# Weight sums for a seven-product up projection: made ahead in DRAM instead of on VectorE, with other banks, buffers and chain slots

## The chip, the cores and the metric

One core of a Trainium2 chip runs the whole program. The metric is the device time of one execution in microseconds (us). TensorE (PE), VectorE (DVE), ScalarE (ACT), GpSimd (POOL) and SyncE (SP) each work through an instruction list of their own, in order, and wait on semaphores; SP and POOL here only issue DMAs.

## The reference

Two transformer blocks are applied to 1024 tokens of width 1024, all in float32. Block one mixes tokens by an RWKV scan and differential attention, block two by a Fourier mix and a gated convolution. The change is in what follows in both of them, and this part reads, in the reference's names:

```
x = x + gt1 * rmsnorm(y, g_post_mix)            # y = mixer output @ w_out
h = modulate(rmsnorm(x, g_pre_ffn), sh2, sc2)   # second block: rmsnorm only
u = dwconv(h @ w_up, ffn_conv) + ffn_conv_b     # w_up is 1024 x 5632, 3 taps over the tokens
val, gate = split(u, 2)                         # second block: gate first, gelu
x = x + gt2 * rmsnorm((val * silu(gate)) @ w_down, g_post_ffn)
```

The first block also needs `silu(c) @ w_mod`, whose later part is summed on DVE while the RWKV scan runs.

## The kernel before, in words

The program is a row of stages: first block's input and projection, the RWKV scan (`rwkv`), attention, and then one long stage with four parts: first mixer (`mixer_out_to_ffn`, "mix1"), its down projection followed by the second block's input jobs and Fourier mix (`DownToMerge`), second mixer ("mix2", the same function), and the last down projection.

Every float32 matmul is done as three: an operand is split into a rounded high part (ACT, `weight_high`, L3402) and the remainder (DVE, `weight_low`, L3407), and high x high, low x high and high x low are added up in PSUM (L3586 to L3588).

A mixer has 186 steps on PE, each with one weight piece of 512 columns (four 128x128 blocks) and 12 matmuls of 512 tokens (24 of 258 in mix2). `plan_steps` writes them down in order:

- Steps 0 to 31, kind "O": 16 output tiles of `w_out`, first token half and then second. For each half a chain of norm work (`chain(a, e)` on PE, ACT and DVE, with e the step counted from the half's start) runs beside the 16 steps that follow: sums of squares, `means`, `spreads`, eight `residual` rows, squares again, `means`, `scale_rows`, and on ACT `shift_rows` (first block only). The chain of half 1 runs beside steps 32 to 47.
- Steps 32 to 47, "early": products P1 and P2 for the eight tiles in `EARLY` = 3, 5, 7, 9, 0, 1, 11, 13. These need only half 0 of h.
- The rest, "late": 22 tiles of h @ w_up, each a value and a gate tile of 128 columns. A tile is computed as a 2x2 block product (tokens and depth each halved) with seven products in place of eight: P1, P6, P7, P5, P2, P4, P3. The early tiles have five left. So there are 8 tiles of five steps and 14 of seven: tiles 0 and 1 have five, tiles 2 to 13 alternate between seven and five, and tiles 14 to 21 have seven.

The seven products want sums and differences of the operands. On the token side they are the "turns" t1 to t4 (`add_turns`, then rounded by `round_turns` on ACT and `low_turns` on DVE), made once before the late steps. On the weight side they are made for every tile on DVE: `add_weights` (L3423, L3425, L3426) and one more sum in `weight_low` (L3415). ACT's `weight_high` of a summed piece waits for the sum.

What a product leaves in PSUM is taken by DVE (`take`, L3856 to L3864, one for each of P6, P7, P5, P4, P3). ACT then scales the centre tap (`centre_gate` after P4's take, `centre_val` after P3's), DVE adds the outer taps (`tap`, L3870), ACT applies the activation, and DVE multiplies (L3888). The result goes to DRAM and is read back for the down projection.

The order of the work is written by hand. At step s, ACT first splits the weights of step s + 3, then does that step's own work; DVE does taps or product, the low split of step s + 3, taps, and last `take(s)`, which waits for PE to end step s. Four ring buffers hold the split weights. Raw weights come in four buffers of 512 KB (8 depth blocks, so a pair of pieces each), loaded by SP and freed after the last use. PSUM banks of the late steps are fixed by kind (`late_bank`): P7 and P4 of a tile share a bank, so P4 waits until DVE has taken P7 (`took`), and PE cannot start P4 until then. PE waits for `w_low` before every step.

## Time and profile before

| | us |
|---|---|
| median of 3 runs | 3728.32 (3721.13 to 3732.64) |
| the profiled execution | 3724.28 |
| its span in the trace | 3722.4 |

| engine | busy us | share of span | instructions |
|---|---|---|---|
| PE | 3406.6 | 92% | 30711 |
| DVE | 2404.7 | 65% | 3809 |
| ACT | 1582.8 | 43% | 2735 |
| POOL | 182.5 | 5% | 335 |

The median of the runs is the time to be compared; the profiled execution, 4.04 us below it, is where all durations below come from. Its span leaves out 1.88 us around it. The page gives busy time by engine, the span in 40 slices with the granted clock of TensorE, the chain of work that ended last, and the costliest groups of instructions with the idle time before them and what ended it. A matmul's listed duration overlaps the next one's, so the pace of PE is read from start to start, and its idle time from the bracket ahead of a matmul.

In time the parts lie about so: RWKV scan 490 to 1010, attention to 1300, mix1 1300 to 1980, down projection to 2250, second block's input and Fourier mix to 2770, mix2 to 3440, last down projection to the end. In the RWKV stage's window the DMA engines are busy for a share of 0.32; the busiest of the page's 40 slices moved 262 GB/s.

### The profile page before, as it was taken

What the parts mean: (1) busy time and instruction counts of PE and PEld (TensorE: products, weight loads), DVE (VectorE), ACT (ScalarE), POOL (GpSimd) and SP (SyncE); (2) the same over time, 40 slices, a digit from 0 to 9 for tenths busy, and PEclk for the clock granted to TensorE, in tenths of its full rate; (3) what the DMA queues carried; (4) which work ended last, traced back from release to release, by engine and by line L of the source; (5) the groups of instructions that cost most, each with busy time, mean ns of one, the idle gap of its engine ahead of it and who ended that gap; (6) DMA issues with size and microseconds to landing.
All of it is one profiled execution on the core that took longest, in us unless ns stands there. A gap on an engine that the chain in (4) does not pass through costs nothing.

```text
span 3722.4 us, 73022 instructions
## 1 busy us (share of the span) xinstructions
PE 3406.6 (92%) x30711; PEld 3081.6 (83%) x30711; DVE 2404.7 (65%) x3809; ACT 1582.8 (43%) x2735; POOL 182.5 (5%) x335
## 2 busy tenths in 40 slices
PE   7999999999989897788898999999999788898999
PEld 4787789888877775666668999899999788898999
DVE  5477778878757746777776884322235777777565
ACT  4556644444347634333334553111134333334454
POOL 2000000000000010000000111000000000000110
PEclk9999999999889999899999999999999899999999
DMA  6234442323233052222325763111123222232774
GB/s 241 71 128 139 140 163 97 112 92 96 55 74 87 1 162 87 63 68 79 95 69 192 262 216 122 29 35 46 49 85 117 80 70 84 69 91 84 261 239 159
DMA packets 328479, 410.36 MB, mean 110 GB/s; under 512 B 15795, under 2 KB 255894, under 8 KB 328152
## 3 DMA queue, kind: packets, MB, share of 16 engines
q1 hardware_dynamic: 298184, 306.49, 26.9%
q0 software_dynamic: 29968, 99.19, 8.2%
q8 instruction: 244, 4.00, 0.5%
q14 instruction: 83, 0.68, 0.1%
HBM read 322.68 MB, written 82.94 MB: 109 GB/s over the span
## 4 chain that ended last, share of the span: by engine, by line
PE 38%; DVE 14%; issue 4%; DVEq 3%; ACT 3%; DMA 2%; ACTq 0%; POOL 0%
PE psum L3586 5%; PE psum L3588 4%; PE psum L3587 4%; PE psum L2846 4%; PE psum L2847 4%; PE psum L2848 4%; PE psum L2369 3%; PE psum L2371 3%; PE psum L2370 3%; DVE mix_u_val L3870 3%; DVE mix_u_gate L3870 2%; DMA down_w_raw<-in_w_down 2%; DVE mix_w_split L3407 2%; ACT mix_w_split L3402 2%; PE psum L2705 1%
## 5 line engine op out<-in xcount | busy, mean ns | idle before, releaser
L2235 DVE TENSOR_TENSOR down_w_lo<-down_w_raw,down_w_hi 128x1024 fp32r<-128x1024 f32 x228 | 270.5, 1186 | 442.2 <-ACT down_w_hi L2209 440.1
L3586 PE MATMUL psum<-mix_t_hi,mix_w_split 128*128 128x258 f32 (+1 forms) x1056 | 358.2, 339 | 145.6 <-DVE mix_x_gate L3858 86.2
L2209 ACT ACTIVATE down_w_hi<-down_w_raw 128x1024 fp32r<-128x1024 f32 x228 | 234.6, 1029 | 572.0 <-PE psum L2848 328.4
L2369 PE MATMUL psum<-down_ghi,down_w_hi 128*128 128x256 f32 x1408 | 404.5, 287 | 12.4 <-DVE down_glo L2240 12.2
L2371 PE MATMUL psum<-down_glo,down_w_hi 128*128 128x256 f32 x1408 | 399.7, 284 | 0.0
L2370 PE MATMUL psum<-down_ghi,down_w_lo 128*128 128x256 f32 x1408 | 399.5, 284 | 0.0
L3586 PEld LDWEIGHTS psum<-mix_t_hi,mix_w_split 128*128 128x128 f32 x1056 | 211.0, 200 | 180.7 <-DVE mix_w_split L3407 106.1
L3587 PE MATMUL psum<-mix_t_hi,mix_w_split 128*128 128x258 f32 (+1 forms) x1056 | 351.2, 333 | 0.0
L3588 PE MATMUL psum<-mix_t_lo,mix_w_split 128*128 128x258 f32 (+1 forms) x1056 | 350.8, 332 | 0.0
L3407 DVE TENSOR_TENSOR mix_w_split<-mix_w_raw,mix_w_split 128x512 fp32r<-128x512 f32 x240 | 165.1, 689 | 212.2 <-ACT mix_w_split L3402 211.9
L2369 PEld LDWEIGHTS psum<-down_ghi,down_w_hi 128*128 128x128 f32 x1408 | 271.6, 193 | 14.5 <-DVE down_glo L2240 14.1
L2370 PEld LDWEIGHTS psum<-down_ghi,down_w_lo 128*128 128x128 f32 x1408 | 271.8, 193 | 0.3
L2371 PEld LDWEIGHTS psum<-down_glo,down_w_hi 128*128 128x128 f32 x1408 | 271.5, 193 | 0.0
L2846 PE MATMUL psum<-h_hi,down_w_hi 128*128 128x348 f32 (+2 forms) x768 | 249.1, 324 | 0.6 <-DVE h_lo L2533 0.6
L2847 PE MATMUL psum<-h_hi,down_w_lo 128*128 128x348 f32 (+2 forms) x768 | 247.1, 322 | 0.0
L2848 PE MATMUL psum<-h_lo,down_w_hi 128*128 128x348 f32 (+2 forms) x768 | 246.9, 321 | 0.0
L3588 PEld LDWEIGHTS psum<-mix_t_lo,mix_w_split 128*128 128x128 f32 x1056 | 210.4, 199 | 17.5
L3587 PEld LDWEIGHTS psum<-mix_t_hi,mix_w_split 128*128 128x128 f32 x1056 | 211.3, 200 | 15.9
L3402 ACT ACTIVATE mix_w_split<-mix_w_sum 128x512 fp32r<-128x512 f32 x132 | 82.4, 624 | 315.4 <-DVE mix_w_sum L3426 242.2
L757 PE MATMUL psum<-h_hi,w_hi 128*128 128x512 f32 (+1 forms) x536 | 209.3, 390 | 0.7 <-DVE w_lo L923 0.7
L758 PE MATMUL psum<-h_hi,w_lo 128*128 128x512 f32 (+1 forms) x536 | 199.4, 372 | 0.0
L759 PE MATMUL psum<-h_lo,w_hi 128*128 128x512 f32 (+1 forms) x536 | 199.3, 372 | 0.0
(501 smaller groups left out, 8676.5 us busy)
## 6 DMA issues: line engine op xcount, KB each, us to landing
down_w_raw<-in_w_down SPq DMA_DIRECT2D x176, 512.0 KB, 4.3
mix_w_raw<-in_w_up SPq DMA_DIRECT2D x104, 512.0 KB, 5.3
g_scratch<-mix_u_val POOLq DMA_DIRECT2D x44, 512.0 KB, 4.0
down_w_raw<-in_w_in SPq DMA_DIRECT2D x36, 512.0 KB, 4.0
down_g_part<-g_scratch POOLq DMA_DIRECT2D x6, 2816.0 KB, 17.2
rw_operands<-step_set SPq DMA_DIRECT2D x16, 1024.0 KB, 6.4
mod_w<-in_w_mod POOLq DMA_DIRECT2D x32, 512.0 KB, 5.6
mix_w_raw<-in_w_out SPq DMA_DIRECT2D x32, 512.0 KB, 4.0
```

Source lines behind the costliest of these rows:

```text
L2209: self.nc.scalar.activation(self.hi[s][:, 0:w], self.raw[s][:, 0:w], ACT.Copy).then_inc(self.w_high, 1)
L2235: last = self.nc.vector.tensor_tensor(self.lo[s][:, 0:w], self.raw[s][:, 0:w], self.hi[s][:, 0:w].bitcast(F32), ALU.subtract)
L2369: nc.tensor.matmul(out, w_hi[:, w], g_hi[:, :], start=(n == 0 and c % 2 == 0), stop=False, skip_group_check=True)
L2370: nc.tensor.matmul(out, w_lo[:, w], g_hi[:, :], start=False, stop=False, skip_group_check=True)
L2371: last = nc.tensor.matmul(out, w_hi[:, w], g_lo[:, :], start=False, stop=(n == KF - 1), skip_group_check=True)
L2846: nc.tensor.matmul(out, w_hi[:, w], x_hi[:, xk, x], start=(kk == 0), stop=False)
L2847: nc.tensor.matmul(out, w_lo[:, w], x_hi[:, xk, x], start=False, stop=False)
L2848: last = nc.tensor.matmul(out, w_hi[:, w], x_lo[:, xk, x], start=False, stop=end)
L3407: nc.vector.tensor_tensor(ring[s % 4][:, 1, :], src, ring[s % 4][:, 0, :].bitcast(F32), ALU.subtract).then_inc(w_low.sem, 1)
L3586: nc.tensor.matmul(out, w[:, 0, c], xh[:, x], start=(first and kk == 0), stop=False, skip_group_check=True)
L3587: nc.tensor.matmul(out, w[:, 1, c], xh[:, x], start=False, stop=False, skip_group_check=True)
L3588: last = nc.tensor.matmul(out, w[:, 0, c], xl[:, x], start=False, stop=(kk == 3), skip_group_check=True)
```

## The change

Five things are changed, all for both mixers.

1. Four sums of `w_up` (1024 x 2816 each in use: 512 rows) are made by DMA in DRAM, in tensors `up_sums`. `sum_weights` issues them on POOL: 16 copies of 1408 KB, then 16 transfers of 1408 KB that add to what they write (`accum_op=ALU.add`), with waits on semaphores between dependent ones. Mixer 0's 32 transfers stand one behind each of the 32 loads of `w_mod` in the RWKV stage; mixer 1's stand behind the tables of the Fourier mix, ahead of POOL's last wait before mix2. DVE's four weight sums per tile are gone. SP waits for all sums of its mixer before the first late load.
2. Raw weights come one piece per step (256 KB) in ten buffers, instead of two pieces in four: 186 loads per mixer instead of 68.
3. The late steps' PSUM banks are handed out by longest unused (`slot_of`, `freed_by`) among all eight (four pairs in mix2).
4. The final rows of half 0 are written where t1 and t4 will be made (`final`) and stay there whole, so that `add_turns` has four additions for each kk instead of six.
5. The chain of half 1 has two residual rows per step (e = 3 to 6) and its own slots: second `means` at e = 8 (before 11), `scale_rows` at e = 10 and 11 (before 13 and 14), `add_turns` spread over e = 11 to 14 (before all of it at 14 and 15), and `low_turns` one kind per step from e = 15 on (before three kinds at e = 15).

The semaphores of the down projection's first rows are also cut from five to three.

```diff
@@ rwkv, gpsimd
                 pool.dma_start(k.mod_w[i % 3][:, :], w_mod[:, kk, c:c + MOD_COLS]).then_inc(mod_landed[i % 3], 16)
+                sum_weights(pool, k, 0, i)
@@ DownToMerge.gpsimd
+        for i in range(32):
+            sum_weights(pool, self.k, 1, i)
         pool.wait_ge(self.used, self.total)
@@
+def sum_weights(pool, k, mixer, at):
+    j, c = divmod(at, 4)
...
+    if j < 4:
+        src = (w[low, gate], w[low, val], w[low, val], w[high, val])[j]
+        pool.dma_start(sums[j, low, :], src).then_inc(done, 16)
+    elif j < 6:
+        src = (w[high, gate], w[low, gate])[j - 4]
+        pool.wait_ge(done, base + 64)
+        pool.dma_start(sums[(0, 2)[j - 4], low, :], src, accum_op=ALU.add, max_dma_last_dim=5632).then_inc(done, 16)
+    else:
+        pool.wait_ge(done, base + 16 * j)
+        pool.dma_start(sums[(1, 3)[j - 6], low, :], sums[(0, 1)[j - 6], low, :],
+                       accum_op=ALU.add, max_dma_last_dim=5632).then_inc(done, 16)
@@ mixer_out_to_ffn
+    for s in range(first_late, STEPS):
+        kind, i = steps[s]
+        if kind in ("P2", "P3"):
+            slot = slot_of["P1" if kind == "P2" else "P5", i]
+        else:
+            slot = min(range(SLOTS), key=lambda j: last_use[j])
+            freed_by[kind, i] = user.get(slot)
...
     def weight_high(act, s):
-        kind, i = steps[s][0:2]
-        src, r = source(s)
-        if kind in SUM and not early(s):
-            act.wait_ge(*w_added.at(4 * i + SUM[kind]))
-        else:
-            act.wait_ge(*w_landed[r % 4].at(landed_at(r)))
+        act.wait_ge(*w_landed[s % RAWS].at(landed_at(s)))
...
     def weight_low(dve, s):
-        if s + 1 < STEPS and s + 1 >= first_late:
-            kind, i = steps[s + 1]
-            if kind == "P6":
-                add_weights(dve, i)
-            elif kind == "P4":
...
     def sync(sp):
-        for r in range(TILES):
-            if r >= 4:
-                sp.wait_ge(*w_low.at(released[r - 4]))
+        for s in range(STEPS):
+            if s >= RAWS:
+                sp.wait_ge(*w_low.at(s - RAWS + 1))
...
+            if s == first_late:
+                for done in k.sums_done:
+                    sp.wait_ge(done, 128 + 128 * spec["mixer"])
@@ tensor, bank_free
-            elif kind == "P4":
-                pe.wait_ge(*took.at(5 * i + 2))
...
+            elif not early(s) and kind != "P2" and freed_by[kind, i]:
@@ vector, chain of half 1
+            elif a == 1:
+                if 3 <= e <= 6:
+                    residual(a, 2 * e - 6, 2 * e - 5)
+                elif e == 8:
+                    means(a, 1)
+                elif e in (10, 11):
+                    scale_rows(a, 4 * e - 40)
+                    if e == 11:
+                        add_turns(0)
+                elif 12 <= e <= 14:
+                    add_turns(e - 11)
+                elif e == 15:
+                    low_turns("t2")
@@ vector, add_turns
-            tt(f["t1"], h0[0][kk][:, :].bitcast(F32), b12, ALU.subtract)
+            tt(f["t1"], f["t1"], b12, ALU.subtract)
             tt(f["t3"], b12, b22_row, ALU.subtract)
-            dve.drain()
-            tt(f["t1"], f["t1"], h0[1][kk][:, :].bitcast(F32), ALU.add)
```

On DVE, in a late tile of seven steps, from one pair of value taps to the gate taps (mix_w_split is the split weights' ring, mix_w_sum the weight sums, mix_u and mix_x_* what is taken from PSUM). Before:

```order
L3870 SCALAR_TENSOR_TENSOR mix_u_val<-mix_x_val_18160,prm,mix_u_val 128x1024 x2
L3407 TENSOR_TENSOR mix_w_split_18167<-mix_w_raw_18164,mix_w_split_18167 128x512
L3415 TENSOR_TENSOR mix_w_sum_18171<-mix_w_raw_18164,mix_w_sum_18171 128x512
L3856 TENSOR_TENSOR mix_u_18151<-psum,mix_x_val_18161 128x512
L3888 TENSOR_TENSOR mix_u_val<-mix_u_val,mix_u_gate 128x1024
L3407 TENSOR_TENSOR mix_w_split_18168<-mix_w_raw_18165,mix_w_split_18168 128x512
L3858 TENSOR_TENSOR mix_x_gate<-mix_u_18151,psum 128x512
L3407 TENSOR_TENSOR mix_w_split_18169<-mix_w_sum_18171,mix_w_split_18169 128x512
L3860 TENSOR_TENSOR mix_x_gate<-mix_x_gate,psum 128x512
L3407 TENSOR_TENSOR mix_w_split_18166<-mix_w_raw_18162,mix_w_split_18166 128x512
L3423 TENSOR_TENSOR mix_w_sum_18170<-mix_w_raw_18163 128x512
L3425 TENSOR_TENSOR mix_w_raw_18163<-mix_w_raw_18163,mix_w_raw_18162 128x512
```

And in the changed kernel:

```order
L3877 SCALAR_TENSOR_TENSOR mix_u_val<-mix_x_val_18211,prm,mix_u_val 128x1024 x2
L3434 TENSOR_TENSOR mix_w_split_18224<-mix_w_raw_18214,mix_w_split_18224 128x512
L3863 TENSOR_TENSOR mix_u_18202<-psum,mix_x_val_18212 128x512
L3895 TENSOR_TENSOR mix_u_val<-mix_u_val,mix_u_gate 128x1024
L3434 TENSOR_TENSOR mix_w_split_18225<-mix_w_raw_18215,mix_w_split_18225 128x512
L3865 TENSOR_TENSOR mix_x_gate<-mix_u_18202,psum 128x512
L3434 TENSOR_TENSOR mix_w_split_18226<-mix_w_raw_18216,mix_w_split_18226 128x512
L3867 TENSOR_TENSOR mix_x_gate<-mix_x_gate,psum 128x512
L3434 TENSOR_TENSOR mix_w_split_18223<-mix_w_raw_18217,mix_w_split_18223 128x512
L3434 TENSOR_TENSOR mix_w_split_18224<-mix_w_raw_18218,mix_w_split_18224 128x512
```

The order of splits, takes and taps is the same; the weight sums (L3415, L3423, L3425, and L3426 just behind) are no longer between them.

On DVE at the end of mix1's early steps, from the first four scaled rows (L3776, now L3783) on; mix_t_sum and mix_t_lo are the turns and their low parts. Before, after all four kk:

```order
L3799 TENSOR_TENSOR mix_t_sum<-mix_y_18148,mix_t_sum 128x512
L3801 TENSOR_TENSOR mix_t_sum<-mix_h_18116,mix_t_sum 128x512
L3803 TENSOR_TENSOR mix_t_sum<-mix_t_sum,mix_h_18116 128x512
L3812 TENSOR_TENSOR mix_t_lo<-mix_t_sum,mix_t_hi 128x512 x4
L3812 TENSOR_TENSOR mix_t_lo<-mix_t_sum,mix_t_hi_18123 128x512
L3812 TENSOR_TENSOR mix_t_lo<-mix_t_sum,mix_t_hi_18124 128x512
L3812 TENSOR_TENSOR mix_t_lo<-mix_t_sum,mix_t_hi_18125 128x512
L3812 TENSOR_TENSOR mix_t_lo<-mix_t_sum,mix_t_hi_18126 128x512
L3812 TENSOR_TENSOR mix_t_lo<-mix_t_sum,mix_t_hi 128x512 x4
L3407 TENSOR_TENSOR mix_w_split_18169<-mix_w_raw_18163,mix_w_split_18169 128x512
```

In the changed kernel:

```order
L3801 TENSOR_TENSOR mix_t_sum<-mix_t_sum,mix_y_18199 128x512
L3802 TENSOR_TENSOR mix_t_sum<-mix_y_18199 128x512
L3804 TENSOR_TENSOR mix_t_sum<-mix_y_18199,mix_t_sum 128x512
L3806 TENSOR_TENSOR mix_t_sum_18176<-mix_t_sum_18176,mix_t_sum 128x512
L3434 TENSOR_TENSOR mix_w_split_18225<-mix_w_raw_18213,mix_w_split_18225 128x512
L3815 TENSOR_TENSOR mix_t_lo<-mix_t_sum,mix_t_hi 128x512 x4
L3434 TENSOR_TENSOR mix_w_split_18226<-mix_w_raw_18214,mix_w_split_18226 128x512
L3815 TENSOR_TENSOR mix_t_lo<-mix_t_sum,mix_t_hi 128x512 x4
```

The low parts of one kind of turn now stand between two weight splits, where before twelve stood in a row ahead of one.

On POOL in the RWKV stage (mod_w are the three buffers of `w_mod` pieces), the start of the changed kernel's list; before, only the L1289 rows stand there:

```order
L1289 DMA mod_w_4212<-in_w_mod 128x1024
L3265 DMA up_sums<-in_w_up 128x2816
L1289 DMA mod_w_4213<-in_w_mod 128x1024
L3265 DMA up_sums<-in_w_up 128x2816
L1289 DMA mod_w_4214<-in_w_mod 128x1024
L3265 DMA up_sums<-in_w_up 128x2816
```

Each load of `w_mod` now has a transfer of 1408 KB ahead of it in POOL's queue.

## Rows read from the trace of the kernel before

**Rows 1.** What PE waited for, 1300:2000, then 2760:3450: us in total, times, longest
```profile
PE psum L3586 <- DVE mix_x_gate L3858: 47.4, 19, 5.7
PE psum L3586 <- ACT mix_x_val L3680: 23.8, 1, 23.8
...
PE psum L3586 <- ACT mix_x_val L3680: 22.6, 1, 22.6
```
**Rows 2.** Timeline of PE in mix1: start, us, engine, line, operands, count, [idle before]
```profile
1656.39 0.77 PE L3586 MATMUL psum<-mix_t_hi,mix_w_split 128*128 128x512 f32 x1 [5.28 <-DVE mix_x_gate L3858]
...
1661.65 0.63 PE L3586 MATMUL psum<-mix_b_hi,mix_w_split 128*128 128x512 f32 x1
...
1855.10 0.40 PE L3586 MATMUL psum<-mix_b_hi,mix_w_split 128*128 128x512 f32 x1
...
1863.50 0.40 PE L3586 MATMUL psum<-mix_t_hi,mix_w_split 128*128 128x512 f32 x1
```
**Rows 3.** Timeline of DVE, one late tile of seven steps in mix1
```profile
1844.56 2.64 DVE L3870 SCALAR_TENSOR_TENSOR mix_u_val<-mix_x_val,prm,mix_u_val 128x1024 f32<-128x1024 f32 x2
...
1847.90 0.69 DVE L3415 TENSOR_TENSOR mix_w_sum<-mix_w_raw,mix_w_sum 128x512 f32<-128x512 f32 x1
...
1854.15 0.69 DVE L3423 TENSOR_TENSOR mix_w_sum<-mix_w_raw 128x512 f32<-128x512 f32 x1
...
1856.93 0.69 DVE L3407 TENSOR_TENSOR mix_w_split<-mix_w_sum,mix_w_split 128x512 fp32r<-128x512 f32 x1 [0.70 <-ACT mix_w_split L3402]
...
1860.24 0.69 DVE L3407 TENSOR_TENSOR mix_w_split<-mix_w_raw,mix_w_split 128x512 fp32r<-128x512 f32 x1 [1.83 <-ACT mix_w_split L3402]
...
1867.07 2.64 DVE L3870 SCALAR_TENSOR_TENSOR mix_u_val<-mix_x_val,prm,mix_u_val 128x1024 f32<-128x1024 f32 x2
```
**Rows 4.** The chain that ended last: first gate tap of tiles 1, 13, 21; mix2's 1, 21
```profile
1536.53 1.28 DVE mix_u_gate L3870
...
1793.52 1.28 DVE mix_u_gate L3870
...
1971.07 1.28 DVE mix_u_gate L3870
...
2997.19 1.28 DVE mix_u_gate L3870
...
3432.19 1.28 DVE mix_u_gate L3870
```
**Rows 5.** Timelines of PE, then DVE, where mix1's late steps begin
```profile
1495.80 0.77 PE L3586 MATMUL psum<-mix_t_hi,mix_w_split 128*128 128x512 f32 x1 [23.76 <-ACT mix_x_val L3680]
...
1463.94 0.69 DVE L3407 TENSOR_TENSOR mix_w_split<-mix_w_sum,mix_w_split 128x512 fp32r<-128x512 f32 x1 [0.79 <-ACT mix_w_split L3402]
...
1469.42 0.69 DVE L3407 TENSOR_TENSOR mix_w_split<-mix_w_raw,mix_w_split 128x512 fp32r<-128x512 f32 x1 [2.21 <-ACT mix_w_split L3402]
...
1483.10 0.69 DVE L3794 TENSOR_TENSOR mix_t_sum<-mix_h,mix_y 128x512 f32<-128x512 f32 x1
...
1487.57 0.69 DVE L3794 TENSOR_TENSOR mix_t_sum<-mix_h,mix_y 128x512 f32<-128x512 f32 x1
...
1516.73 2.65 DVE L3870 SCALAR_TENSOR_TENSOR mix_u_gate<-mix_x_gate,prm,mix_u_gate 128x1024 f32<-128x1024 f32 x2
```
**Rows 6.** Timeline of POOL in the RWKV stage: loads 15 and 31 of 0 to 31
```profile
710.58 0.53 POOL L1289 DMA_DIRECT2D mod_w<-in_w_mod  x1 [25.26 <-DVE mod_sum L1575]
...
919.33 0.53 POOL L1289 DMA_DIRECT2D mod_w<-in_w_mod  x1 [21.19 <-DVE mod_sum L1575]
```
**Rows 7.** Timeline of POOL, the end of the Fourier tables and mix2's first loads
```profile
2764.11 2.15 POOL L3451 DMA_DIRECT2D mix_temp<-x_scratch  x4 [480.23 <-PE psum L2848]
```
**Rows 8.** DMA issues of the page: count, KB each, median us from issue to landing
```profile
mix_w_raw<-in_w_up SPq DMA_DIRECT2D x104, 512.0 KB, 5.3
...
mod_w<-in_w_mod POOLq DMA_DIRECT2D x32, 512.0 KB, 5.6
...
dft_cos<-in_dft_cos_k POOLq DMA_DIRECT2D x1, 1042.0 KB, 6.7
```

More of the change, by code:

```diff
@@ L2138, in __init__ @@
         self.part_rows = [k.at(f"{name}_part_rows{s}", [20, PART], (86528, 43136)[s]) for s in range(2)]
-        self.first_landed = [sem(f"{name}_first_rows_landed{j}") for j in range(5)]
+        self.first_landed = [sem(f"{name}_first_rows_landed{j}") for j in range(3)]
         self.part_landed = [None] + [sem(f"{name}_part_landed{p}") for p in range(1, SEQ // PART)]
@@ L3250 @@
     pass
+def sum_weights(pool, k, mixer, at):
+    j, c = divmod(at, 4)
+    w, active_first = ((k.ins["w_up"][0], False), (k.ins["w_up_2"][0], True))[mixer]
+    val, gate = (slice(FF, 2 * FF), slice(0, FF)) if active_first else (slice(0, FF), slice(FF, 2 * FF))
+    sums, done, base = k.up_sums[mixer], k.sums_done[c], 128 * mixer
+    low, high = slice(P * c, P * c + P), slice(512 + P * c, 512 + P * c + P)
+    if j < 4:
[9 more added lines that the diff above has]
+                       accum_op=ALU.add, max_dma_last_dim=5632).then_inc(done, 16)
 class Counted:
@@ L3320, in mixer_out_to_ffn @@
     xv = lambda i: stash[X_BUFFER[i]]
-    fresh = [i for i in range(KF) if i not in EARLY]
-    kept_before = lambda i: max([QUEUE] + [KEPT[j] + 1 for j in fresh if j <= i - SETS])
     low_cols, high_cols = slice(dst, dst + n), slice(dst + n, dst + 2 * n)
@@ L3428, in sync @@
-    def sync(sp):
-        for r in range(TILES):
-            if r >= 4:
-                sp.wait_ge(*w_low.at(released[r - 4]))
-            elif before and r < 2:
-                sp.wait_ge(before.low, before.total - 1 + r)
+        nc.vector.tensor_tensor(ring[s % 4][:, 1, :], raw[s % RAWS][:, :], ring[s % 4][:, 0, :].bitcast(F32),
+                                ALU.subtract).then_inc(w_low.sem, 1)
+    def sync(sp):
+        for s in range(STEPS):
+            if s >= RAWS:
+                sp.wait_ge(*w_low.at(s - RAWS + 1))
+            elif before and s < 4:
+                sp.wait_ge(before.low, before.total - 1 + s // 2)
@@ L3569, in tensor @@
             a, e = chain_of(s)
-            first = kind in ("P1", "P6", "P7", "P5") or (kind == "O" and steps[s][2] == 0)
+            first = kind not in ("P2", "P3") and (kind != "O" or steps[s][2] == 0)
             for j in range(nb):
@@ L3574, in tensor @@
                 else:
-                    out = k.psum[:, late_bank(i, BANK[kind], j), 0:pw]
+                    out = k.psum[:, late_bank(i, kind, j), 0:pw]
                 if kind == "P2":
@@ L3777, in scale_rows @@
                 else:
-                    nc.vector.scalar_tensor_tensor(out=row, in0=row, scalar=gain_pre(order[a][j]), in1=spread_out[:, 0:n],
+                    nc.vector.scalar_tensor_tensor(out=final(a, order[a][j]), in0=row, scalar=gain_pre(order[a][j]), in1=spread_out[:, 0:n],
                                                    op0=ALU.mult, op1=ALU.mult).then_inc(scaled.sem, 1)
@@ L3951, in four_tiles, with mixer_memory @@
     return [k.at(f"{name}{j}", [n], places[j], dt)[:, :] for j in range(4)]
-def mixer_memory(k, name, n, first, ring_at, spots):
+def mixer_memory(k, name, n, first, ring_at, first_spots, later_spots):
     at = k.at
@@ L3959, in mixer_memory @@
     h0 = [[first_rows[:, kk // 4, q, kk % 4, :] for kk in range(KD)] for q in range(2)]
-    spots = iter(spots)
+    first_spots, later_spots = iter(first_spots), iter(later_spots)
     turn, turn_f32 = {}, {}
-    for which in ("t1", "t2", "t3", "t4", "b22"):
-        places = [[next(spots) for _ in range(4)] for _ in range(2)]
+    for which in ("t1", "t4", "t2", "t3", "b22"):
+        lasting = which in ("t1", "t4")
+        places = [[next(first_spots if lasting and q else later_spots) for _ in range(4)] for q in range(2)]
         turn[which] = [four_tiles(k, f"{name}_{which}_{p}", n, places[q], F32R) for q, p in enumerate(("hi", "lo"))]
@@ L4089, in program @@
         k.x_dram = nc.dram_tensor("x_scratch", [KD, P, SEQ], F32, kind="Internal").ap()
+        k.up_sums = [nc.dram_tensor(f"up_sums{m}", [4, 512, FF], F32, kind="Internal").ap() for m in range(2)]
+        k.sums_done = [k.lasting(f"up_sums_done{c}") for c in range(4)]
         k.g_dram = nc.dram_tensor("g_scratch", [KF, P, SEQ], F32, kind="Internal").ap()
```

213 lines of the change are left out of this document (95 added, 118 removed).

## The prediction

> **What bounds the kernel now.** I read the busy shares first: PE is at 92%, so the gain can only lie in its gaps. The windows by part show where they are: the late steps of both mixers and the passage into them. PE's waits name the cause [rows 1]: in mix1 47.4 us for L3858, DVE's take of P7, and one wait of 23.8 us as the late steps begin; in mix2 the latter is 22.6. P4 uses P7's bank and stands behind that take, and the take stands behind taps and splits in DVE's list, so the question is who sets the pace, the bank or DVE.
>
> PE's own pace: 36 matmuls (three steps) lie between the last two rows of [rows 2], 8.40 us, 0.233 each (the 2.4 GHz level), so a step is 2.80 us, a tile of seven 19.6, a tile of five 14.0. The chain that ended last shows the real pace [rows 4]: tiles 1 to 13, six pairs of a seven and a five, take 257.0 us, 42.8 a pair where PE needs 33.6; tiles 13 to 21 take 177.55 us, 22.2 each where PE needs 19.6. Tiles 1 to 21 take 434.5 us in mix1 and 435.0 in mix2.
>
> DVE's timeline of a seven-step tile [rows 3] has a period of 22.51 us, and DVE waits in it only for ACT: 0.70 us once and 1.83 us twice. The 1.83 is a loop: take, ACT's centre tap, ACT's high split, DVE's low split, and nothing in DVE's list lies between. DVE is the bound, and the waits of [rows 1] are how PE learns of it.
>
> **The late steps.** Removed on DVE per tile: L3415, 0.78 us to the next start, and from 1854.15 to the split at 1856.93, 2.78 us of three sums and the 0.70 wait for the last [rows 3]. Together 3.56.
> - Seven steps: 22.51 - 3.56 = 18.95 us of DVE, under PE's 19.6. PE becomes the bound. DVE may fall some 6 us behind inside a tile (gate taps and both loops come at its end), but splits are made three steps = 8.4 us ahead, so this is just covered. I take 19.65 a tile: tiles 13 to 21 take 157.2 us, 20.3 less.
> - A pair: 42.8 less twice 2.95 us of sums (2.17 for the three, 0.78) and about 0.5 of waits for them leaves 36.4, over PE's 33.6. DVE stays the bound, since both loops stay in the five-step tile, and PE idles some 2.8 us a pair. Six pairs: 218.4 us, 38.6 less.
> - Tile 0 to 1: 19.8 us ([rows 4, 5]) becomes about 17.5, 2.3 less.
> That is 61 in mix1. Mix2's matmuls are 516 columns a step against 512, so PE's part is 1% longer and I take 59.
>
> The new banks remove the wait by name, not the bound: a bank is reused four steps or more later in mix2, nine or more in mix1 after tile 1, and a split that PE needs for step s is in DVE's list behind the take of step s - 4. So the bank wait costs nothing, and gives nothing beyond the DVE time counted.
>
> **The passage into the late steps.** Before, PE ended its early steps and idled 23.76 us, to 1495.80 [rows 5]. DVE's chain slot with the first scaled rows begins at 1463.94 and lasts 5.48 us to 1469.42 (shift on ACT, then its split); it leads to PE's start 31.9 us later. Six additions of a kk took 4.47 us (1483.10 to 1487.57); four take about 3.1. In the changed list, from the same slot on: 5.5, then 6.4 (four rows, additions of one kk, split), three times 3.85, and 1.4 for a split and the first low part of t2: 24.8 us. But the slot now comes at e = 10, with six steps of PE's left, 17.0 us with a spread, where it came with three. It can begin 1.0 us after that step. So PE idles 25.8 - 17.0 = 8.8 us. What PE did for sums in steps 10 and on moves ahead, so the slot starts 1.8 us later against the old place than the steps alone say: P6 starts at about 1479.9, 15.9 us earlier. Tile 0 then has one kind of low turns per step and is paced by DVE at about 4 us a step, as long as before to its gate taps. In mix2, which has no shift on ACT, the idle of 22.6 becomes about 8, and tile 0 gets some 3 shorter: 17. Two residual rows per step cost nothing themselves (3.5 us of DVE in a step of PE's of 2.8 us and two sums); what they bring is the earlier slot.
>
> **Loads.** Seven loads of 256 KB per tile replace two of 512 KB. A 512 KB load takes 5.3 us to land [rows 8]; ten buffers let a load start some six steps, 16 us, before ACT wants it. Nothing on the path. At 2.65 us each one after the other, seven would take 18.6 of 19.6 us, so only if nothing overlapped would this be near. By the Trainium skill ("DMA: Bandwidth & Descriptors", Anatomy of one DMA) a DMA costs about 2.0 us fixed plus bytes at 436 GB/s: an estimate by it is 2.6 us for 256 KB, the same answer. No run here shows 256 KB of `w_up` alone.
>
> **The sums by DMA.** No row shows an accumulating or a DRAM to DRAM transfer. For 1408 KB, bounds by the nearest rows: 1042 KB landed in 6.7 us, 512 KB in 5.6 [rows 8], so 9.1 to 15.4 for a move of that size with its latency, and up to twice the lower, 18.1, if an addition reads a second stream at that pace. Below, latency is paid once in a full queue: 1408 KB at the 262 GB/s of the profile's busiest slice is 5.5. I take 9 for an addition, nearest to the 1042 KB row, and 6 for a copy.
>
> Mixer 0: the 16 additions go with loads 16 to 31 of `w_mod`, from 710.58 to 919.33 [rows 6], 208.7 us, beside 16 loads of some 2.5 us of queue time. No delay up to (208.7 - 40) / 16 = 10.5 us an addition, about 11.8 with the loads' lead of one pair (some 20 us). With 9 the cost is nothing; the DMA engines are busy for only 32% of that window. I put 3 us on contention with the scan's loads. Could it gain? No, nothing is taken out there.
>
> Mixer 1: POOL was idle for 480.23 us before its loads of x at 2764.11 [rows 7]. 16 copies of 6 and 16 additions of 9 are 240 us. Hidden up to about (480 - 96) / 16 = 24 us an addition. The weight loads beside them, one of at most 512 KB per job of some 11 us, are issued two jobs ahead, so even twice their time to land is covered.
>
> **Sum.** 3724.28 - (15.9 + 61) - (17 + 59) + 3 = 3574. The median of the runs lies 4 above the profiled execution, so 3578, 4.0% less than 3728.
>
> **Rivals.**
> 1. PE gains only half of it. Late tiles of seven steps have 0.65 us of slack against DVE; if their stalls do not vanish, and PE falls to half clock after each stall of a pair, the gain melts. Behind a stall of 5.28 us 12 matmuls took 5.26 us, 0.44 each (the 1.2 GHz level), against 0.233 [rows 2]: 2.4 us more, and for each of 12 pairs 29 us. With 0.7 us more in each of 28 seven-step tiles, 20 us, this gives about 3578 + 49 = 3627. For it: that stall comes in a pair of tiles, and pairs keep a stall. Against it: by the sum it is 2.8 us and not 5.28, and DVE sets the pair's length, so a slower PE is partly hidden.
> 2. The additions are slow and hold up the scan: slower than before. POOL's queue is first in, first out, so a load of `w_mod` stands behind an addition; DVE's mod sums wait for it, and with them in DVE's list the scan. Each us over 11.8 costs 16. At 18.1 us (the bound above) it is 100 us, 3678; from 21.2 us on the change loses, and at 24, 195 us, the time is 3773. For it: twice the reading and an addition in the DMA engine, with no row that says otherwise. Against it: bytes alone give 9. The Trainium skill ("DMA: Bandwidth & Descriptors", Queues, rings and completion order) has descriptors of one ring consumed in order, which is the rule this rests on; that no later load overtakes is not shown in this trace.
> 3. The seven-product steps are held by the weights from DRAM: SP's wait for `sums_done` before the first late load. In mix2, at more than 24 us an addition, both x and late weights come late. It joins rival 2.
>
> **Chances.** Forecast 0.66, rival 1 0.21, rival 2 (with 3) 0.13, of which 0.08 is slower than before and 0.05 lies between. 3578 is the forecast's; its own range is 3555 to 3605. The range for 8 in 10 goes to rival 1: 3548 to 3642. Runs of this kernel tell 0.3% (11 us) from no change: faster 0.90, same 0.02, slower 0.08.
>
> **What would show it.** Right: gate taps 19.6 to 19.8 us apart in tiles 14 to 21 and 36 to 37 a pair; no wait for a take, but waits for the low split (now L3434), in five-step tiles; one wait of 7 to 10 us where P6 begins; the scan's stage still 520 us long; POOL past its additions before 2764. Wrong: DVE waiting for `mod_w` or DMA issues on POOL stretched after 710 (rival 2); PE stalls over 3 us with matmuls 0.43 us apart in each pair (rival 1); tiles of seven above 20.3.

## The result, and the profile after

| | us |
|---|---|
| changed kernel, median of 4 runs | 3829.07 (3825.76 to 3833.37) |
| kernel before, beside them, median of 4 runs | 3730.48 |
| ratio | 1.0268, 95% interval 1.0245 to 1.0291 |
| span of the profiled execution | 3827.1 (before 3722.4) |

The change makes the kernel 2.7% slower; 4.0% faster was forecast. The span cut at five instructions that all kernels here have shows where it went. The marks are DVE's first product of the attention stage, ACT's first weight split of mix1, PE's first transposition of the meta rows (some 10 us behind mix1's last gate row), ACT's first split of mix2, and SP's last store. In brackets stands the time between the stores of gate rows 0 and 21, the late steps.

| kernel | to the attention | attention | mix1 (late) | down, second input | mix2 (late), last down |
|---|---|---|---|---|---|
| before | 1056.8 | 249.3 | 685.2 (450.6) | 766.9 | 959.3 (451.1) |
| after | 1179.7 | 248.0 | 623.3 (406.9) | 876.8 | 894.9 (405.0) |
| difference | +122.9 | -1.3 | -61.9 | +109.9 | -64.4 |

So the mixers gained 126 us of the 153 forecast, and the two places where the sum transfers run, costed at 3 us together, lost 233. The windows by part show the same (us, busy time of each engine with its instructions, granted clock, DMA share, GB/s), of the kernel before:
```profile
485.00:1010.00 525.00, 488.02 (x11926) 460.75 (x11925) 407.67 (x905) 216.84 (x576) 16.93 (x32) 0.95 0.32 103
...
2250.00:2500.00 250.00, 250.00 (x1495) 233.39 (x1496) 82.50 (x127) 52.45 (x78) 9.57 (x17) 1.00 0.17 52
```
and of the changed one:
```profile
485.00:1134.00 649.00, 518.80 (x11962) 488.99 (x11962) 405.63 (x901) 213.62 (x578) 43.30 (x64) 0.87 0.53 153
...
2311.00:2600.00 289.00, 192.59 (x1050) 174.71 (x1049) 60.39 (x108) 39.72 (x66) 34.13 (x49) 0.82 0.75 195
2600.00:2940.00 340.00, 339.87 (x2148) 339.66 (x2147) 87.69 (x87) 61.44 (x71) 2.20 (x4) 1.00 0.17 48
```
In the scan the instructions are nearly the same and the stage is 124 us longer, at a DMA share of 0.53 where it was 0.32. In the second block's input part PE, busy all the time before, idles 96 of 289 us, while the 32 transfers of mixer 1 run; once they are through, it is at 100% again.

**What waits there.** First the waits of the scan window, then those of the input part (us in total, times, longest):
```profile
POOL mod_w L1289 <- DVE mod_sum L1576: 353.6, 25, 35.6
...
ACT kb L1728 <- DMA unit<-rw_values: 135.8, 12, 16.5
ACT kb L1728 <- DMA unit_first<-rw_values: 51.3, 6, 15.7
```
```profile
DVE down_w_lo L2236 <- ACT down_w_hi L2210: 191.3, 10, 40.5
ACT down_w_hi L2210 <- DMA down_w_raw<-in_w_in: 109.8, 4, 38.8
...
PE psum L2849 <- DVE down_w_lo L2236: 35.8, 1, 35.8
```
POOL waits for DVE, as before [rows 6]; DVE never waits for `mod_w`. The scan waits for its own operands, which SP loads: 18 waits, 187 us, where the kernel before had 5 and 5.6 us. These loads have a short lead (the time from issue to need), as one of them shows: SP's issue, then ACT's first use, before:
```profile
606.91 0.62 SPq L1254 DMA_DIRECT2D unit_first<-rw_values  x1
...
612.41 0.63 ACT L1727 ACTIVATE kb<-unit_first 128x512 f32<-128x512 f32 x1 [0.44 <-DMA unit_first<-rw_values]
```
after:
```profile
626.67 1.08 SPq L1254 DMA_DIRECT2D unit_first<-rw_values  x1
...
640.88 0.63 ACT L1728 ACTIVATE kb<-unit_first 128x512 f32<-128x512 f32 x1 [9.15 <-DMA unit_first<-rw_values]
```
In both, ACT is ready for the load some 5 us after its issue (5.5 - 0.44 and 14.2 - 9.15), so whatever it takes beyond that is waited for. The DMA issues of the scan window (count, KB each, median us to landing), before (`mod_w` is in [rows 8]):
```profile
unit<-rw_operands SPq DMA_DIRECT2D x22, 512.0 KB, 5.0
...
unit<-rw_values SPq DMA_DIRECT2D x26, 128.0 KB, 5.9
```
after:
```profile
up_sums<-in_w_up POOLq DMA_DIRECT2D x24, 1408.0 KB, 12.4
mod_w<-in_w_mod POOLq DMA_DIRECT2D x32, 512.0 KB, 7.3
unit<-rw_operands SPq DMA_DIRECT2D x22, 512.0 KB, 16.4
up_sums<-up_sums POOLq DMA_DIRECT2D x8, 1408.0 KB, 16.9
...
unit<-rw_values SPq DMA_DIRECT2D x26, 128.0 KB, 15.7
```
and in the input part after, 2311 to 2600:
```profile
up_sums<-in_w_up POOLq DMA_DIRECT2D x24, 1408.0 KB, 41.0
up_sums<-up_sums POOLq DMA_DIRECT2D x8, 1408.0 KB, 29.1
down_w_raw<-in_w_in SPq DMA_DIRECT2D x12, 512.0 KB, 37.9
```
of which the kernel before, 2285 to 2760, had:
```profile
down_w_raw<-in_w_in SPq DMA_DIRECT2D x28, 512.0 KB, 4.0
```
What is on POOL's own queue suffers little (5.6 to 7.3 us). What SP issues beside it does: a unit's 512 KB take 16.4 us instead of 5.0, its 128 KB 15.7 instead of 5.9, and a block of `w_in` 37.9 instead of 4.0.

**The late steps.** Two timelines of one pair in mix1 (start, us, engine, line, operands, idle before), PE, then DVE:
```profile
1709.44 0.39 PE L3589 MATMUL psum<-mix_t_lo,mix_w_split 128*128 128x512 f32 x1
1713.38 0.77 PE L3587 MATMUL psum<-mix_b_hi,mix_w_split 128*128 128x512 f32 x1 [3.54 <-DVE mix_x_gate L3867]
...
1718.62 0.39 PE L3587 MATMUL psum<-mix_h,mix_w_split 128*128 128x512 f32 x1
```
```profile
1709.84 0.69 DVE L3865 TENSOR_TENSOR mix_x_gate<-mix_u,psum 128x512 f32<-128x512 f32 x1
1710.62 1.23 DVE L3895 TENSOR_TENSOR mix_u_val<-mix_u_val,mix_u_gate 128x1024 f32<-128x1024 f32 x1
1711.76 0.69 DVE L3434 TENSOR_TENSOR mix_w_split<-mix_w_raw,mix_w_split 128x512 fp32r<-128x512 f32 x1
1712.54 0.69 DVE L3867 TENSOR_TENSOR mix_x_gate<-mix_x_gate,psum 128x512 f32<-128x512 f32 x1
```
and the stores of gate rows 1, 13, 14 and 21, which close a tile:
```profile
1651.12 0.54 POOL L3469 DMA_DIRECT2D g_scratch<-mix_u_val  x1 [15.96 <-DVE mix_u_val L3895]
...
1885.05 0.53 POOL L3469 DMA_DIRECT2D g_scratch<-mix_u_val  x1 [16.23 <-DVE mix_u_val L3895]
1907.22 0.53 POOL L3469 DMA_DIRECT2D g_scratch<-mix_u_val  x1 [21.64 <-DVE mix_u_val L3895]
...
2041.46 0.53 POOL L3469 DMA_DIRECT2D g_scratch<-mix_u_val  x1 [15.57 <-DVE mix_u_val L3895]
```
Tiles 13 to 21 take 156.4 us (177.55 in [rows 4]), 19.60 each between rows 14 and 20: PE's own pace. The six pairs take 233.9 (257.0), 39.0 each. The stall of [rows 2] is no longer P4 behind P7's take: it is P3, which adds into P5's bank and cannot start before P5's take (L3867). That wait was there before too, nearly all of it hidden behind the other (1520 to 1800 of the kernel before, P5's take being L3860 there):
```profile
PE psum L3586 <- DVE mix_x_gate L3860: 3.1, 6, 0.5
```
The 12 matmuls behind the new stall take 5.24 us instead of 2.80, at 0.43 each (the 1.2 GHz level). What PE waited for, 1420 to 2041:
```profile
PE psum L3587 <- DVE mix_x_gate L3867: 24.0, 7, 4.6
...
PE psum L3587 <- DVE mix_t_lo L3815: 7.7, 2, 7.3
```
The 7.3 is the passage, 23.8 before [rows 1, 5].

### The profile page after: what moved, and what is told of

It is laid out like the page before. It is cut to its first block, busy times and chain, and to the rows that moved or that the text cites. A ratio compares the mean times of both kernels' runs of the same rounds, so it can differ in the third digit from the quotient of the medians.

```text
span 3827.1 us, 72929 instructions
## 1 busy us (share of the span) xinstructions
PE 3424.5 (89%) x30711; PEld 3114.0 (81%) x30711; DVE 2276.1 (59%) x3617; ACT 1580.3 (41%) x2735; POOL 234.1 (6%) x399
## 4 chain that ended last, share of the span: by engine, by line
PE 45%; DVE 6%; issue 3%; DMA 3%; ACT 2%; another core or an unknown queue 2%; DVEq 2%; ACTq 0%; POOL 0%
PE psum L3587 8%; PE psum L3588 7%; PE psum L3589 7%; PE psum L2849 4%; PE psum L2850 4%; PE psum L2851 4%; PE psum L2370 3%; PE psum L2372 3%; PE psum L2371 3%; DMA down_w_raw<-in_w_down 1%; DMA down_w_raw<-in_w_in 1%; DVE mix_u_val L3877 1%; DVE mix_u_gate L3877 1%; PE psum L3488 1%
## 5 line engine op out<-in xcount | busy, mean ns | idle before, releaser
L3434 DVE TENSOR_TENSOR mix_w_split<-mix_w_raw,mix_w_split 128x512 fp32r<-128x512 f32 x372 | 255.4, 688 | 296.1 <-ACT mix_w_split L3430 295.8
L2370 PE MATMUL psum<-down_ghi,down_w_hi 128*128 128x256 f32 x1408 | 404.1, 287 | 11.7 <-DVE down_glo L2241 11.5
L3587 PE MATMUL psum<-mix_t_hi,mix_w_split 128*128 128x258 f32 (+1 forms) x1056 | 339.9, 322 | 13.7 <-DVE mix_t_lo L3815 13.6
L3588 PE MATMUL psum<-mix_t_hi,mix_w_split 128*128 128x258 f32 (+1 forms) x1056 | 339.3, 321 | 0.0
L3589 PE MATMUL psum<-mix_t_lo,mix_w_split 128*128 128x258 f32 (+1 forms) x1056 | 339.0, 321 | 0.0
L3430 ACT ACTIVATE mix_w_split<-mix_w_raw 128x512 fp32r<-128x512 f32 x372 | 228.0, 624 | 155.7 <-PE psum L3589 134.4
L2370 PEld LDWEIGHTS psum<-down_ghi,down_w_hi 128*128 128x128 f32 x1408 | 271.4, 193 | 13.7 <-DVE down_glo L2241 13.3
L3587 PEld LDWEIGHTS psum<-mix_t_hi,mix_w_split 128*128 128x128 f32 x1056 | 200.5, 190 | 31.6 <-DVE mix_w_split L3434 14.6
L3588 PEld LDWEIGHTS psum<-mix_t_hi,mix_w_split 128*128 128x128 f32 x1056 | 200.5, 190 | 16.0
L3589 PEld LDWEIGHTS psum<-mix_t_lo,mix_w_split 128*128 128x128 f32 x1056 | 200.3, 190 | 16.2
L2849 PEld LDWEIGHTS psum<-h_hi,down_w_hi 128*128 128x128 f32 x768 | 148.4, 193 | 76.5 <-issue 40.4
```

What stands on the lines that cost most here:

```text
L2370: nc.tensor.matmul(out, w_hi[:, w], g_hi[:, :], start=(n == 0 and c % 2 == 0), stop=False, skip_group_check=True)
L2849: nc.tensor.matmul(out, w_hi[:, w], x_hi[:, xk, x], start=(kk == 0), stop=False)
L3434: nc.vector.tensor_tensor(ring[s % 4][:, 1, :], raw[s % RAWS][:, :], ring[s % 4][:, 0, :].bitcast(F32), ALU.subtract).then_inc(w_low.sem, 1)
L3587: nc.tensor.matmul(out, w[:, 0, c], xh[:, x], start=(first and kk == 0), stop=False, skip_group_check=True)
L3588: nc.tensor.matmul(out, w[:, 1, c], xh[:, x], start=False, stop=False, skip_group_check=True)
L3589: last = nc.tensor.matmul(out, w[:, 0, c], xl[:, x], start=False, stop=(kk == 3), skip_group_check=True)
```

## The experiments

Each kernel ran beside the kernel before (3728 to 3731 us), so ratios compare across groups.

| kernel | median us | ratio to before, 95% | to attention | attention | mix1 (late) | down, second input |
|---|---|---|---|---|---|---|
| no_sums | 3604 | 0.9660 (0.9624, 0.9697) | 1066.5 | 248.3 | 621.8 (404.2) | 767.7 |
| no_first_sums | 3712 | 0.9961 (0.9943, 0.9979) | 1057.5 | 247.7 | 623.0 (406.9) | 876.0 |
| attn_paced | 3628 | 0.9735 (0.9705, 0.9766) | 1069.1 | 258.7 | 622.9 (406.5) | 783.4 |
| small_packets | 3673 | 0.9854 (0.9816, 0.9892) | 1114.7 | 249.7 | 622.3 (406.5) | 798.5 |
| fixed_banks | 3632 | 0.9736 (0.9714, 0.9758) | 1062.7 | 258.9 | 623.7 (407.8) | 783.0 |
| late_rows | 3640 | 0.9758 (0.9739, 0.9777) | 1064.6 | 261.4 | 627.9 (403.4) | 784.2 |
| more_dve | 3727 | 0.9992 (0.9981, 1.0004) | 1061.5 | 259.1 | 670.5 (447.6) | 783.7 |
| plain_copies | 3789 | 1.0164 (1.0142, 1.0186) | 1162.2 | 248.2 | 622.2 (404.3) | 856.8 |
| take_first | 3595 | 0.9644 (0.9625, 0.9663) | 1062.1 | 257.7 | 605.5 (387.8) | 784.1 |
| paced_small | 3609 | 0.9687 (0.9661, 0.9713) | 1056.1 | 247.9 | 622.7 (406.7) | 775.8 |
| paced_small_take | 3584 | 0.9614 (0.9591, 0.9637) | 1073.8 | 249.1 | 605.0 (387.8) | 775.7 |
| tiny_packets | 3674 | 0.9854 (0.9833, 0.9875) | 1109.0 | 248.2 | 623.0 (406.8) | 796.0 |

The nine kernels without transfers in the scan reach the first mark between 1056.1 and 1073.8 us, median 1062.7, with the same code up to there: that part is not known better than some 10 us from one profile, and the price of the transfers in it is 117 against that median.

**Is it the transfers, and are the two places separate?** no_sums:
```diff
-                sum_weights(pool, k, 0, i)
...
-        for i in range(32):
-            sum_weights(pool, self.k, 1, i)
...
+        if kind in SUMS and spec["mixer"] in (0, 1):
+            c = (i + side[SUMS.index(kind) // 2]) * P
+            return w_up[:, 0:4, c:c + P] if SUMS.index(kind) % 2 else w_up[:, 4:8, c:c + P]
```


> The changed kernel without its 64 sum transfers: the steps P5, P6, P7 and P3 load blocks of w_up itself (same size and shape of load), so the products of those steps are not of the sums. All else stays: ten load buffers, banks, rows kept, two residual rows a step. Theory (contention: the transfers fill the DMA engines and delay SP's loads): the scan's stage is back at 520 us (649 in the changed kernel) and the second block's input part at 520 (629), the mixers keep their gain, so 3829 - 129 - 110 = 3590, range 3580 to 3605. Rival (something else in the change, the ten smaller loads or the moved buffers, slows the two parts): they stay above 600 us and the time above 3750.

In place of the sums, the late steps then use `w_up` itself, so the products are not those of the block product. no_first_sums is the same for mixer 0 alone.

> Only mixer 0's 32 sum transfers are left out (its late steps load w_up itself instead of the sums); mixer 1's stay where they are. Contention: 129 us less, all in the scan's stage, 3700 (3690 to 3715), and mixer 1's part still 629 us. Rival (the two groups of transfers are one load on DRAM or POOL, and what is left costs more): less than 100 us gained, above 3730.

Both as the theory had it, 14 and 12 us above its numbers. Everything lost comes from the 64 transfers, and it is a matter of the part they stand in: with mixer 0's gone the input part still takes 876.0. With none, the kernel is 3.4% faster than before.

**Does it matter where they stand?** attn_paced puts mixer 0's in the attention stage and spreads mixer 1's:
```diff
@@ rwkv
-                sum_weights(pool, k, 0, i)
@@ attention
+        @block.gpsimd
+        def _(pool):
+            for i in range(32):
+                if i >= 2:
+                    pool.wait_ge(scored[0], i - 1)
+                sum_weights(pool, k, 0, i)
@@ DownToMerge.gpsimd
         for i in range(32):
+            if i >= 2:
+                pool.wait_ge(self.used, DOWN_STEPS + 4 + i * 3 // 2)
             sum_weights(pool, self.k, 1, i)
```


> Complete kernel. Mixer 0's 32 transfers move from the scan's stage to the attention stage (one released per score tile), mixer 1's are released one per 1.5 weight steps of the second block's input part instead of all at once. Contention that costs only where loads have a short lead: scan 520 us, attention 286 to 300 (its loads are a head ahead), input part 520 to 545: 3590 to 3640, taken 3610. Rival 1 (each transfer costs its 3.5 to 4 us wherever it stands, since it takes DMA time that some load wants): 3800 to 3830. Rival 2 (the attention's loads are delayed as the scan's were): attention over 350 us, time 3660 to 3720.

It does: 3628, both rivals fall (3610 was expected). The attention's window, 1069 to 1327, and what its queues did there:
```profile
1069.00:1327.00 258.00, 213.31 (x1418) 184.10 (x1418) 176.45 (x232) 167.52 (x320) 26.01 (x35) 0.94 0.88 238
```
```profile
q0 software_dynamic: 6656, 46.14, 69.1%
...
k_high<-k_scratch SPq DMA_DIRECT2D x14, 320.0 KB, 17.7
k_low<-k_scratch SPq DMA_DIRECT2D x14, 320.0 KB, 19.0
q_both<-q_scratch SPq DMA_DIRECT2D x14, 256.0 KB, 15.4
```
The DMA engines are busier (0.88) than in the scan (0.53), and the stage's loads land as late as the scan's did, 15 to 19 us. Yet it is only 10 us longer. Its loads are issued a head (eight score tiles) ahead, all but the first ones, which PE needs at once. PE waits for a load once in this stage, for those first ones. In the kernel before:
```profile
PE psum L1883 <- DMA k_low<-k_scratch: 6.1, 1, 6.1
```
in attn_paced:
```profile
PE psum L1890 <- DMA k_low<-k_scratch: 15.7, 1, 15.7
```
in paced_small (below), where POOL's first transfer is issued once the first score tile is done:
```profile
PE psum L1890 <- DMA k_low<-k_scratch: 6.6, 1, 6.6
```
That is the 10 us. The later loads land as late and cost nothing. So it isn't the traffic that costs but the traffic beside loads with a short lead. 69.1% of 258 us for 32 transfers is 5.6 us of all 16 engines each.

**What delays a load?** small_packets, and later tiny_packets with 704 for 1408:
```diff
-        pool.dma_start(sums[j, low, :], src).then_inc(done, 16)
+        pool.dma_start(sums[j, low, :], src, max_dma_last_dim=1408).then_inc(done, 16)
...
-                       accum_op=ALU.add, max_dma_last_dim=5632).then_inc(done, 16)
+                       accum_op=ALU.add, max_dma_last_dim=1408).then_inc(done, 16)
```


> The changed kernel, its 64 transfers cut into pieces of 1408 bytes instead of rows of 11264 (copies) and 5632 (additions). If SP's loads are late because each of their small packets stands behind a long one of POOL's queue in the same engine, short ones let them through: scan's unit loads land in 8 us instead of 16, stage 540 to 590 us, time 3700 to 3780. If it is the engines' time in total, it stays 649 and 629 or grows with eight times as many packets: 3830 to 3950.

> The changed kernel with its transfers in pieces of 704 bytes, in their old places (1408 bytes gave 3673 us, rows of 11264 and 5632 gave 3829). If the length of the packet ahead of SP's packets sets the delay, it falls on: unit loads land in 9 to 10 us, 3640 to 3665. If 1408 bytes had already reached what the engines' time in total costs, the same or more, since the transfers take more packets: 3670 to 3760.

The first turns a loss of 2.7% into a gain of 1.5%, more than its expectation had (3700 to 3780); the second brings no more, as its second case had it. In the scan, 485 to 1000, the queue of the transfers, one of their issues and the unit loads, with 1408 bytes:
```profile
q0 software_dynamic: 27136, 62.92, 48.2%
...
up_sums<-in_w_up POOLq DMA_DIRECT2D x24, 1408.0 KB, 14.5
...
unit<-rw_operands SPq DMA_DIRECT2D x20, 512.0 KB, 11.7
```
with 704 bytes:
```profile
q0 software_dynamic: 43520, 62.92, 54.0%
...
up_sums<-in_w_up POOLq DMA_DIRECT2D x24, 1408.0 KB, 14.4
...
unit<-rw_operands SPq DMA_DIRECT2D x20, 512.0 KB, 9.7
```
The transfers themselves become slower (12.4 to 14.5 us) and take more of the engines, and the kernel becomes faster, since SP's loads get through: 16.4, 11.7, 9.7 us. At 704 bytes they land sooner again, but the stage is only 6 us shorter, less than one profile can tell, and the runs show no difference. What still holds it there was not followed further. And the second cut shortened the copies alone: in the traces' records of single packets a copy's are 1408 and 704 bytes long, but an addition's are nearly all 4224 in both kernels.

How long a packet holds an engine is in the same records: in the changed kernel's scan 0.46 us for a copy's 11264 bytes and as much for an addition's 5632, in small_packets 0.13 and 0.18, in tiny_packets 0.08 and 0.18. A unit's 512 KB are 512 packets, 32 for each engine. If each waited for one packet of POOL's, they would land some 15 us later, 4 to 6 and 3 to 6 in the three kernels (an estimate from these figures). Measured, it is 11.4, 6.7 and 4.7 us. The Trainium skill ("DMA: Bandwidth & Descriptors", Queues, rings and completion order, Arbitration) has each DMA engine take turns between the queues by whole packets. By that rule a short packet of SP waits for a long one of POOL each time, and these runs agree with it; they do not show the turns themselves.

**Is adding dearer than copying?** plain_copies was meant to turn all 32 adding transfers into copies. Its edit reaches only the first of the two statements, so 16 are plain and 16 (`up_sums` onto itself) still add:
```diff
-        pool.dma_start(sums[(0, 2)[j - 4], low, :], src, accum_op=ALU.add, max_dma_last_dim=5632).then_inc(done, 16)
+        pool.dma_start(sums[(0, 2)[j - 4], low, :], src, max_dma_last_dim=5632).then_inc(done, 16)
```

> Compared with the changed kernel (3829 us). The 32 adding transfers are plain copies of the same size, pieces and waits, in the same places; so the sums are not made. If adding is what makes the transfers dear (a second read at the target, 9 us taken against 6 for a copy): scan's stage 649 to about 610, input part 629 to about 590, time 3745 to 3790. If a transfer costs by the bytes moved alone: 3815 to 3835.

Yes: 40 us go with half of the adding, 18 in the scan (hardly more than one profile can tell) and 20 in the input part, of the 233 that the transfers cost. What the other half costs was not run. The packet records give the price on the engines: in the changed kernel's scan the 16 copies take 58.4 us of all 16 engines, the 16 additions 117.0, so 3.7 and 7.3 us each, and in plain_copies those 117.0 are 88.0.

**Which part of the change pays in the mixers?** The next three stand on attn_paced. fixed_banks:
```diff
+    FIXED = {"P1": 0, "P6": 1, "P7": 2, "P4": 2, "P5": 3}
+    fixed = lambda i, kind: 4 * ((i + 1) % 2) + FIXED[kind] if nb == 1 else (FIXED[kind] + 2) % 4
...
-            slot = min(range(SLOTS), key=lambda j: last_use[j])
+            slot = fixed(i, kind)
```


> Complete kernel, compared with attn_paced (3628 us). The late steps take the PSUM banks by the fixed table of the kernel before (P4 in P7's bank) instead of the bank longest unused; all else as in attn_paced. Theory of the prediction (DVE sets the pair's length, banks bring nothing): 3625 to 3635. Rival (the bank wait costs PE time of its own, since P4 stands behind P7's take, which stands behind gate taps): each pair 1 to 3 us longer, 3645 to 3670.

late_rows sets the conditions of the second half's chain back to those of the first, with additions and low parts in its last steps:
```diff
@@ the second half's chain on PE, ACT and DVE, at each of the three
-            elif a == 1:
+            elif False:
...
```


> Complete kernel, compared with attn_paced (3628 us). In the second half the residual rows go one per step again and the scaled rows, additions and splits of the turned rows come in the last three early steps, as before; nothing else is undone. Prediction's term: the wait of PE before P6 grows from about 9 us to 24 less what the smaller additions save (3 to 5), so 10 to 15 us in each mixer: 3648 to 3658. Rival (the passage is set by the splits and additions themselves, not by where they start): under 5 us in all, 3628 to 3633.

more_dve:
```diff
+        extra = 0
+        if s >= first_late:
+            extra = {"P6": 3, "P4": 2}.get(steps[s][0], 0)
+        for _ in range(extra):
+            dve.drain()
+            nc.vector.tensor_tensor(spare[:, :], raw[s % RAWS][:, 0:384],
+                                    raw[s % RAWS][:, 0:384], ALU.add)
```


> Complete kernel, compared with attn_paced (3628 us). In each late tile DVE does five sums of 128x384 into a spare buffer, with a drain ahead of each, about 3.0 us where the kernel before had three sums and a take, 3.56 us. Theory (what the mixers gained is DVE's time): seven-step tiles go from 19.6 to about 22, pairs from 39 to 44 or 45, some 45 to 57 us a mixer, time 3720 to 3742. Rival (the gain came from the banks or from the loads, and DVE has slack): under 30 us in all, below 3660.

The banks bring nothing that the runs can tell (3632 for 3628; in mix2's late steps perhaps 5 us, 409.6 for 404.9 in one profile). The DVE time is the gain: about 3.0 us of it a tile give back 99 us, and late steps of 447.6 are nearly those of before (450.6); a pair is 42.8 us again, by the stores of gate rows 1 and 13. The two rows per step and the earlier slots bring little. PE's wait at the passage of mix2, late_rows:
```profile
PE psum L3595 <- DVE mix_t_lo L3828: 12.5, 1, 12.5
```
attn_paced:
```profile
PE psum L3595 <- DVE mix_t_lo L3823: 5.9, 1, 5.9
```
That is 6.6 us (6.4 in mix1, 13.7 for 7.3), and 2 to 3 of it come back in the late steps (403.4 for 406.5). In the runs it is 12 us, and the intervals overlap. The expectation of 20 to 30 was too high.

**What does PE still lose in a pair?** take_first, on attn_paced:
```diff
+            ahead = kind == "P5" and i in EARLY and i > 0
+            if ahead:
+                take(s)          # before the product and the split of this step
...
-            if s >= first_late:
+            if s >= first_late and not ahead:
                 take(s)
```


> Complete kernel, compared with attn_paced (3628 us). In the five-step tiles DVE takes P5 ahead of the product and the weight split of that step instead of behind them. In the changed kernel P3, which adds into P5's bank, waits 3.54 us for that take once a pair (L3867), and the 12 matmuls behind it run 0.43 us apart (1.2 GHz), 2.4 us more: together 5.9 of the 39.1 us of a pair, where 33.6 are matmuls. Theory (this wait, not DVE's total, is what PE still loses): the take comes 2.0 us earlier, so a pair is 37.1 us if the clock still falls and about 34.8 if it does not; 12 pairs: 3604 or 3576. Rival (DVE's total sets the pair, the order is free): 3625 to 3632.

One take moved two instructions forward is worth 33 us. PE, then DVE's take, at the same place:
```profile
1598.55 0.47 PE L3595 MATMUL psum<-mix_b_hi,mix_w_split 128*128 128x512 f32 x1 [1.75 <-DVE mix_x_gate L3875]
...
1601.42 0.40 PE L3595 MATMUL psum<-mix_h,mix_w_split 128*128 128x512 f32 x1
```
```profile
1597.71 0.69 DVE L3875 TENSOR_TENSOR mix_x_gate<-mix_x_gate,psum 128x512 f32<-128x512 f32 x1
```
The stall is 1.75 us instead of 3.54, and behind it 12 matmuls take 2.87 us: the clock stays at its 2.4 GHz level. The six pairs of mix1 save 2.5 us each (36.5 a pair, by the stores), between the two figures of the expectation.

**Together.** paced_small is attn_paced with pieces of 1408 bytes and nothing issued before the attention's second score tile or before step 4 of the input part; paced_small_take adds the take.

> Complete kernel, compared with attn_paced (3628 us). As attn_paced, with the transfers in pieces of 1408 bytes, and none of them ahead of the attention's second score tile or of step 4 of the input part. What attn_paced still pays (attention 258.7 us against 248 to 249, input part 783.4 against 767) is contention with the first loads of each stage and long packets: attention 250, input part 772, time 3605 to 3615. Rival (more packets cost more time wherever they are): 3635 to 3660.

> Complete kernel: both of the two changes above at once. If both theories hold they add: 3555 to 3590. If neither: 3628.

They add up to within 8 us (19 and 33 off 3628 would be 3576): 3584 us, 3.9% faster than the kernel before and 6.4% than the changed one. It is the fastest of all here. And paced_small's 3609 is 5 us from the 3604 without any transfer: cut and paced like this, all 64 cost next to nothing. A fourth buffer for the scan's units, which would lengthen the lead instead, was not tried.

## Why the prediction was wrong

Its step that failed is the term "3 us on contention with the scan's loads", with "even twice their time to land is covered" for the input part: 0 to 3 us were taken, 233 measured. It asked how long a transfer takes and who stands behind it in POOL's queue, and took the DMA share of 0.32 as room. It never asked what becomes of the loads of another queue, and how early these are issued. The transfers were no larger than taken (on the engines 3.7 us for a copy and 7.3 for an addition, against 6 and 9). The scan's unit loads, left out of the working, went from 5.0 to 16.4 us with a lead of 5, and in the input part a block of `w_in` went from 4.0 to 37.9, nine times and not twice.

By its steps:
- **Seven-step tiles, 157.2 us for tiles 13 to 21:** right, 156.4.
- **Pairs, 36.4 us:** 39.0, so 15.6 us too little in mix1. The working took DVE's total as the bound and said that the bank wait gives nothing. Nearly true of the banks (fixed_banks), but P3 adds into P5's bank whatever the table says. Rival 1 had this: a stall a pair, and 2.4 us of half clock behind it, "for each of 12 pairs 29 us". It was given 0.21 and should have been in the sum. take_first shows the wait by itself: 36.5 a pair without most of it.
- **The passage, P6 15.9 us earlier, 17 in mix2:** right. Counted from ACT's first split, P6 starts 15.2 us sooner in mix1 and 15.5 in mix2, gate row 0 16.5 and 16.4, with a wait of 7.3 where 8.8 was expected (5.9 for 8 in mix2). The reason given ("what they bring is the earlier slot") is only half of it: undoing the slot costs 5 to 8 us in mix1. The rest would be the smaller additions from the kept rows; that was not tried alone.
- **Banks nothing, 256 KB loads nothing:** banks shown by fixed_banks. The mixers wait for no load of a late step in the trace, and no_sums with all ten buffers keeps the whole gain. A 256 KB load of `w_up` landed in 3.1 us, where 2.65 was taken. The formula cited beside it from the Trainium skill is stated there for DMAs that GpSimd issues, while SP issues these.
- **Rival 2, the scan held up, slower than before:** right in sign and in one of the two places, wrong in mechanism. Nothing stood behind an addition: POOL waited for DVE. The rule on one ring's order that was cited for it did not decide; the runs agree with the rule on turns between queues in the same section. With 0.08 for slower its chance was far too low, since only this one path to a slow scan was priced.

With the parts of the table in place of the prediction's terms: 3574 + 15.0 + 11.6 (the mixers) + 119.9 + 109.9 (the transfers) - 1.3 = 3829.1. The profiled execution took 3828.93. That this fits is no further proof, since the terms are differences of the same two traces. Nor is it one that paced_small_take, at 3584, lies near the 3578 of the forecast: it has a take moved forward that the forecast did not have.

## What to carry to other kernels

Before a bulk transfer goes into an idle queue, list the loads of all other queues in that window with their lead, and hold it against their time to land beside the bulk (here three times what it was in the scan, nine times with 32 transfers issued at once). A stage whose loads run a head ahead bore a DMA share of 0.88, one with a lead of 5 us not 0.53; if it has to share, cut the bulk into pieces of about the size of the other's packets and release them by the consumer's progress. And when one wait goes, read which other wait stands on the same product and bank: it was hidden, and a stall of 3 to 5 us can cost PE its clock on top.
